# A two-block transformer kernel with split fp32 weights: three raw panel buffers instead of five, ten split ones instead of nine, and MoBA pairs computed in 512 columns

## What is computed

```
# first_block (two layers)
h = x
h = h + rmsnorm(gmlp_mixer(rmsnorm(h)))          # layer 0, stage GMLP
h = h + rmsnorm(conv_ffn(rmsnorm(h)))            # stage FFN0
h = h + rmsnorm(diff_attention(rmsnorm(h)))      # layer 1, stage DIFF
h = h + rmsnorm(conv_ffn(rmsnorm(h)))            # stage FFN1
# second_block
x = h + 0.5 * swiglu(rms_norm(h))                # stage FFN2
u = rms_norm(x) @ w_in                           # stage MIX
x = x + concat(mla_attention(u), moba_attention(u)) @ w_out
x = x + 0.5 * swiglu(rms_norm(x))                # stage FFN3
return rms_norm(x)

def conv_ffn(x):    # D_FF = 2816, causal depthwise conv of 3 taps
    g, u = split(causal_dwconv(x @ w_up))
    return (gelu(g) * u) @ w_down
def swiglu(x):
    return (silu(x @ w_gate) * (x @ w_up)) @ w_down
```

## Time and profile before

| | |
|---|---|
| median of 3 runs | 1059.04 us (1058.21 to 1059.07) |
| profiled execution | 1058.96 us |
| its span | 1056.8 us |
| PE busy | 1048.7 us (99%), 5806 matmuls |
| DVE busy | 776.3 us (73%) |
| ACT busy | 653.1 us (62%) |
| POOL busy | 49.7 us (5%) |
| DMA | 198.11 MB, mean 187 GB/s |
| granted TensorE clock | 1.00 |

### The profile page before, as it was taken

The page is one execution under the profiler, slowest core; times in us unless marked ns, Lnnn a source line. Parts: engine busy times, 40 slices in busy tenths (PEclk is TensorE's granted clock), DMA queues, the critical chain, the costliest instruction groups (busy, mean ns, idle before and its releaser), DMA issues.

```text
span 1056.8 us, 15343 instructions
## 1 busy us (share of the span) xinstructions
PE 1048.7 (99%) x5806; PEld 901.5 (85%) x5806; DVE 776.3 (73%) x1237; ACT 653.1 (62%) x1177; POOL 49.7 (5%) x45
## 2 busy tenths in 40 slices
PE   9999999999999999999999999999999999999997
PEld 7988888888888788888888888888898878888886
DVE  6788977888678889888887656655667867655664
ACT  6777756666667777666567555545556657444553
POOL 1910000000000000000000000000000000000000
PEclk9999999999999999999999999999999999999999
DMA  9764866655564257656554755666355536565641
GB/s 346 265 223 142 248 198 209 220 182 183 181 214 120 93 169 245 202 189 206 193 182 133 263 179 179 204 198 216 101 179 160 180 100 212 189 191 202 203 160 40
DMA packets 56776, 198.11 MB, mean 187 GB/s; under 512 B 6576, under 2 KB 8536, under 8 KB 56704
## 3 DMA queue, kind: packets, MB, share of 16 engines
q1 hardware_dynamic: 56160, 196.42, 56.5%
q10 hardware_dynamic: 432, 0.53, 0.1%
q0 software_dynamic: 112, 0.20, 0.1%
HBM read 195.35 MB, written 1.25 MB: 186 GB/s over the span
## 4 chain that ended last, share of the span: by engine, by line
PE 97%; DVE 1%; ACT 1%; issue 0%; POOL 0%; ACTq 0%; DVEq 0%; POOLq 0%
PE G L1485 31%; PE Y L1577 26%; PE G L1489 16%; PE G L1529 3%; PE G L1538 2%; PE G L1536 2%; PE G L1470 2%; PE Y L1572 2%; PE G L1471 2%; PE G L1472 2%; PE G L1551 1%; PE Y L1471 1%; PE Y L1472 1%; PE Y L1470 1%; PE G L1723 1%; PE Y L1601 1%
## 5 line engine op out<-in xcount | busy, mean ns | idle before, releaser
L928 DVE TENSOR_TENSOR w_low<-raw,w_high 128x1024 fp32r<-128x1024 f32 x346 | 417.4, 1224 | 35.2 <-ACT w_high L473 33.2
L473 ACT CAST w_high<-raw 128x1024 fp32r<-128x1024 f32 x351 | 362.7, 1045 | 13.3 <-DMA raw<-in_panels 8.4
L1485 PE MATMUL G<-x_parts,w_high 128*128 128x512 f32 x1408 | 352.5, 393 | 0.0
L1485 PEld LDWEIGHTS G<-x_parts,w_high 128*128 128x128 f32 x1408 | 257.1, 189 | 49.1 <-issue 0.7
L1489 PEld LDWEIGHTS G<-x_parts,w_low 128*128 128x128 f32 x1408 | 192.2, 191 | 13.7
L1489 PE MATMUL G<-x_parts,w_low 128*128 128x256 f32 x1408 | 196.4, 283 | 0.0
L574 ACT COPY big<-G 128x512 f32<-128x512 f32 x80 | 46.8, 585 | 226.4 <-PE G L1489 226.4
L1031 DVE TENSOR_TENSOR w<-G,big 128x512 f32<-128x512 f32 x80 | 55.2, 690 | 155.9 <-ACT big L574 155.8
L1577 PE MATMUL Y<-w_high,a_high 128*128 128x512 f32 x416 | 130.9, 396 | 1.0 <-DVE a_low L1297 1.0
L1577 PE MATMUL Y<-w_high,a_low 128*128 128x512 f32 x416 | 128.9, 391 | 0.0
L1577 PE MATMUL Y<-w_low,a_high 128*128 128x512 f32 x416 | 128.6, 390 | 0.0
(11 more groups left out here) (273 smaller groups left out, 1157.1 us busy)
## 6 DMA issues: line engine op xcount, KB each, us to landing
raw<-in_panels SPq DMA_DIRECT2D x352, 512.0 KB, 4.3
gain_pre<-in_gains SPq DMA_DIRECT2D x7, 512.0 KB, 5.5
gain_post<-in_gains SPq DMA_DIRECT2D x4, 512.0 KB, 6.4
big<-in_xT SPq DMA_DIRECT2D x4, 256.0 KB, 7.7
h<-in_x SPq DMA_DIRECT2D x2, 512.0 KB, 8.3
big<-rel_rows SPq DMA_DIRECT2D x8, 128.0 KB, 4.8
big<-in_w_s SPq DMA_DIRECT2D x1, 512.0 KB, 9.1
big<-in_b_s SPq DMA_DIRECT2D x1, 512.0 KB, 10.8
```

Source lines behind the costliest of these rows:

```text
L473: s.copy(WH[:, n % RING, :], raw[:, n % RAWS, :]).then_inc(hi, 1)
L928: v.tensor_tensor(WL[:, n % RING, :], raw[:, n % RAWS, :], WH[:, n % RING, :].bitcast(F32), ALU.subtract).then_inc(lo, 1)
L1485: mm(out, WH[:, n % RING, k * P:(k + 1) * P], X2[:, k, :, :], start=k == 0, stop=False, skip_group_check=True)
```

## The change

What it does:

1. `RAWS` goes from 5 to 3 and `RING` from 9 to 10. `load(n)` so waits for the split of panel n - 3, and the cast of panel n for PE's use of panel n - 10.
2. The cap of `share` goes up by one: 9 panels ahead on ACT, 8 on DVE. For the last eight features it is RING as before, now 10 and 9.
3. Panel DIFF+29 is split by POOL instead of DVE. POOL's helper falls in two, `at_boundary` with the wait on the rows and `low_part` without.
4. In the tail of DIFF the order on ACT and DVE is another: `upto(DIFF + 29)` on ACT comes before the squares of heads 6 and 7, `head_values(7)` on DVE before `low_head(4)`, and the last panels are cast one head later or earlier.
5. The MoBA q/k pairs go through `wide_tile` (banks G[:, 0] and G[:, 1]), and through `low_qk` on ACT and `sum_qk` on DVE. `qk_out` and its semaphore are gone, and the waits on it are waits on `dsum_r`. The banks of the latent queries, keys and values are renumbered.

The diff, cut to this:

```diff
-RAWS = 5
-RING = 9
+RAWS = 3
+RING = 10
...
-        BY_POOL = [STARTS[b] + 3 for b in range(1, 7)]
+        BY_POOL = [STARTS[b] + 3 for b in range(1, 7)] + [DIFF + 29]
...
-            def low_part(b):
-
-                n = STARTS[b] + 3
-                pool.wait_ge(xn_r, sixth(b, 0, 2))
+            def low_part(n):
                 pool.wait_ge(lo, n)
                 pool.wait_ge(hi, n + 1)
                 g.tensor_tensor(WL[:, n % RING, :], raw[:, n % RAWS, :], WH[:, n % RING, :].bitcast(F32),
                                 ALU.subtract).then_inc(lo, 1)
 
-            low_part(1)
+            def at_boundary(b):
+
+                pool.wait_ge(xn_r, sixth(b, 0, 2))
+                low_part(STARTS[b] + 3)
+
+            at_boundary(1)
             pool.wait_ge(rel_rd, 16 * 8)
             g.tensor_copy(bias[:, :, 0:P], bias[:, :, SC - P:SC]).then_inc(bias_r, 1)
-            for b in range(2, 7):
-                low_part(b)
+            at_boundary(2)
+            low_part(DIFF + 29)
+            for b in range(3, 7):
+                at_boundary(b)
...
-                todo = min(seen + (8 if f < NF - 8 else RING), PANELS - 1) + 1 - made[0]
+                todo = min(seen + (9 if f < NF - 8 else RING), PANELS - 1) + 1 - made[0]
...
 
-                act.wait_ge(used, DIFF + 9 + 2 * k + m)
+                act.wait_ge(used, (DIFF + 9 if k < HEADS else MIX - 5) + 2 * k + m)
                 if k:
                     act.wait_ge(dsum_r, 2 * (k - 1) + m + 1)
                 s.activation(qk_low[:, m, :], G[:, m, T:2 * T], ACT.Copy, scale=1.0 if m else DIFF_D ** -0.5)\
                     .then_inc(dlow_r, 1)
-
-            def qk_out(a):
-                act.wait_ge(used, MIX - 4 + 2 * a)
-                bank = G[:, (a - 7) % 2, :]
-                s.activation(qk[:, a % 2, 0, :], bank[:, 0:T], ACT.Copy, scale=DIFF_D ** -0.5)
-                s.copy(qk[:, a % 2, 1, :], bank[:, T:2 * T]).then_inc(qk_r, 1)
 
...
+            upto(DIFF + 29)
             high_head(3)
             squares_out(6).then_inc(ac, 1)
             rms_out(6, 7, 3)
-            high_head(4)
-            upto(DIFF + 29)
+            high_head(4), high_head(5)
             squares_out(7).then_inc(ac, 1)
             rms_out(7, HEADS, 4)
-            high_head(5)
+            upto(DIFF + 30)
+            high_head(6)
             upto(DIFF + 31)
-            for e in range(6, HEADS):
-                high_head(e)
-                upto(DIFF + 26 + e)
+            high_head(7)
+            upto(DIFF + 33)
 
             boundary(3, ACT.Gelu_apprx_tanh)
...
+            low_qk(9, 0)
             upto(B + 17)
-            qk_out(9)
-            turned_out(8, 0), turned_out(8, 1)
+            low_qk(9, 1)
+            turned_out(8, 0)
+            low_qk(10, 0)
+            turned_out(8, 1)
             upto(B + 18)
-            exps(9)
-            qk_out(10)
+            exps(9, lambda: low_qk(10, 1))
             cast(8)
...
             upto(B + 19)
             turned_out(9, 1)
             upto(B + 20)
             exps(10)
+            low_qk(11, 0)
             cast(9)
             upto(B + 21)
-            qk_out(11)
+            low_qk(11, 1)
...
-                s.activation(mlaV[:, t, :], G[:, 1 - t, :], ACT.Copy, scale=rtc[:, 2 + t:3 + t]).then_inc(mlav_r, 1)
+                s.activation(mlaV[:, t, :], G[:, t, :], ACT.Copy, scale=rtc[:, 2 + t:3 + t]).then_inc(mlav_r, 1)
...
-                todo = min(seen + (7 if f < NF - 8 else RING - 1), PANELS - 1) + 1 - made[0]
+                todo = min(seen + (8 if f < NF - 8 else RING - 1), PANELS - 1) + 1 - made[0]
...
             norm_head(5)
+            head_values(7)
             low_head(4)
             inverse_rms(6, 7, 3)
             norm_head(6)
-            head_values(7)
-            upto(DIFF + 29)
             low_head(5)
...
             dve.wait_ge(cb_r, 1)
+            sum_qk(9, 0)
+            upto(B + 16)
+            sum_qk(9, 1)
             upto(B + 17)
+            sum_qk(10, 0)
 
...
-                if a < HEADS:
+                if a < 12:
                     pe.wait_ge(dsum_r, 2 * a + 2)
-                elif a < 12:
-                    pe.wait_ge(qk_r, a - HEADS + 1)
...
-                if j < 2:
-                    pe.wait_ge(v_r, 6 - j)
-                else:
-                    pe.wait_ge(qk_r, j - 1)
                 for m in range(2):
-                    tile_out(B + 10 + 2 * j + m, G[:, (j + 1) % 2, m * T:(m + 1) * T])
+                    if j:
+                        pe.wait_ge(dsum_r, 2 * (HEADS + j - 1) + m + 1)
+                    else:
+                        pe.wait_ge(v_r, 5 + m)
+                    wide_tile(B + 10 + 2 * j + m, G[:, m, :])
                     if m == 0 and between is not None:
                         between()
 
...
-                    pe.wait_ge(qk_r, 3 + u)
+                    pe.wait_ge(dsum_r, 2 * HEADS + 7 + u)
                 else:
```

More of the change, by code:

```diff
@@ L242, in build_program @@
         ah, al = sem("a_high_r"), sem("a_low_r")
-        v_r, qk_r, sc_r, nm_r, ex_r, at_r, T_r, pt_r, pv_r, ov_r, ss_r, ot_r = (
-            sem(n) for n in ("v_r", "qk_r", "scores_r", "negmax_r", "exp_r", "attn_r", "turned", "turned_r",
+        v_r, sc_r, nm_r, ex_r, at_r, T_r, pt_r, pv_r, ov_r, ss_r, ot_r = (
+            sem(n) for n in ("v_r", "scores_r", "negmax_r", "exp_r", "attn_r", "turned", "turned_r",
                              "pv_r", "ov_r", "ss_r", "out_turned"))
@@ L853, in _ @@
             upto(B + 15)
-            qk_out(8)
+            low_qk(8, 0), low_qk(8, 1)
             act.wait_ge(cms, 1)
@@ L1120, in combine, with pair_weights @@
                 v.tensor_reduce(nm[:, b, 2:4], out[:, :, P:SC], AX_X, ALU.max, negate=True).then_inc(nm_r, 1)
-            def pair_weights(a):
+            def pair_weights(a, between=None):
                 b = a % 2
@@ L1131, in pair_weights @@
                     last.then_inc(an_r, 1)
+                    if m == 0 and between is not None:
+                        between()
             def weigh(a):
@@ L1382, in _ @@
             upto(B + 14)
+            sum_qk(8, 0), sum_qk(8, 1)
             dve.wait_ge(cl_r, 5)
@@ L1419, in _ @@
             upto(B + 18)
-            pair_weights(9)
+            pair_weights(9, lambda: sum_qk(10, 1))
             combine(10)
@@ L1424, in _ @@
             pair_weights(10)
+            sum_qk(11, 0)
             low_out(9)
             upto(B + 21)
+            sum_qk(11, 1)
             queries(0)
@@ L1920, in mla_q @@
                             ready(n)
-                        last = product(G[:, (7 + u) % 2, m * T:(m + 1) * T], n % RING, blk % 8 * P, P,
+                        last = product(G[:, u % 2, m * T:(m + 1) * T], n % RING, blk % 8 * P, P,
                                        CH[k], CL[k], k == 0, k == 2)
@@ L1937, in mla_k @@
                     for k in range(2):
-                        last = product(G[:, (11 + u) % 2, m * T:(m + 1) * T], n % RING,
+                        last = product(G[:, u % 2, m * T:(m + 1) * T], n % RING,
                                        ((u % 2 * 2 + m) * 2 + k) * P, P, CH[3 + k], CL[3 + k],
@@ L1951, in mla_v @@
                         hic, loc = WH[:, j, half(k)], WL[:, j, half(k)]
-                        mm(G[:, 1 - t, :], xh, hic, start=k == 0, stop=False)
-                        mm(G[:, 1 - t, :], xh, loc, start=False, stop=False)
-                        last = mm(G[:, 1 - t, :], xl, hic, start=False, stop=k == 1)
+                        mm(G[:, t, :], xh, hic, start=k == 0, stop=False)
+                        mm(G[:, t, :], xh, loc, start=False, stop=False)
+                        last = mm(G[:, t, :], xl, hic, start=False, stop=k == 1)
                 last.then_inc(used, 1)
```

4 lines of the change are left out of this document (2 added, 2 removed).

## The result

The changed kernel took **1147.36 us** in the median of 4 runs (1146.45 to 1152.58), against 1059.05: 1.0844 times as long, with a 95% interval of 1.0831 to 1.0857, or 88 us slower. Medians and differences in this document leave out two runs that fell in a slower state, one of 1256.51 us (experiment 7) and one of 3702.28 us (experiment 11). The prediction had the sign and the kind of loss right (1105, range 1068 to 1128), but about half its size: the result lies outside the range.

What follows compares the result with a forecast made beforehand. PE was taken to bound the kernel, 99% busy. Terms 1.5 + 17.2 + 2 + 0 + 17.2 + 2.2 + (4.6 - 0.9) + 2.2 = +46.0 us on about 1059 gave 1105 us, range 1068 to 1128.

Steps and rivals of the forecast that it cites:

- The bound and the loop: Whole kernel and conv FFNs: PE bounds before; three raw buffers close a loop through ACT, DVE and SP's loads, 8.8 us.
- 0.5 us per step more than PE's 8.31: Conv FFN steps of three panels: the raw loop sums to 8.86, called 8.8 us, so each step loses this.
- The size of a conv FFN: FFN0 and FFN1: late start plus accumulating loops, less end slack, cost 17.2 us each.
- From there I add loops: FFN0 from the split at 116.7: 4 x 6.5, 7 x 8.8, 10.1 and 6 x 8.8 lead to 267.2.
- slack at the end: End of a conv FFN: PE's last d panel began 1.55 us after the last hidden low part, taken off 18.7.
- one cast's worth, 10.1: Conv FFN step f = 14: the cap grows by one, two casts stand ahead of the tap, step 10.1 us.
- bounds: nothing, and one landing of 3.5: Start of GMLP: fourth load behind the first split, two parts of x behind that load; taken as +1.5 us.
- The stop for the latent values: MIX: load of B+30 waits for the split of B+27, so PE waits for the mlaV copies, +4.6 us.
- The SwiGLU FFNs: FFN2 and FFN3: only the start is late; PE's g(4) waits 2.2 us for the sum of f = 2 in each.
- late copy of `first_two`: Start of FFN0: ACT's second such copy stands behind a late cast and PE waits for it, about 1 us.
- The clock: Whole kernel, rival, chance 0.11: granted clock falls after about ten PE stops, +28 us on top, 1133 us.
- The tail of DIFF and the pairs: DIFF's tail: -0.9 and about +1.0, together 0; MoBA pairs in MIX: eight panels by `wide_tile`, -0.9 us.

Runs made afterwards that it cites:

- experiment 7: Kernel before with five raw buffers, but loads of GMLP's panels wait for the split of n - 3 as if three: 1070.35 us, 1.0107.
- experiment 11: Kernel before with the MoBA pairs in 512 columns, plus share's caps raised to 9 and 8, five raw buffers: 1060.38 us, 1.0015.
- experiment 5: Changed kernel with last tap and hidden tile's high part ahead of all casts of the step on ACT in conv FFNs: 1107.76 us, 1.0468.
- experiment 13: Changed kernel itself, unedited, run again beside another run on the same chip: 1146.65 us.
- experiment 12: Changed kernel with unread matmuls filling PE's idle time in FFN0 and FFN1, ahead of g(4) and the waits for f = 20 and 21: 1149.28 us, 1.0865.
- 14: Changed kernel with 9 unread matmuls ahead of PE's waits for hidden tiles f = 19 and 20 in both conv FFNs: 1149.16 us.

## Why the prediction was wrong, point by point

- **The bound and the loop: right.** "0.5 us per step more than PE's 8.31" was 8.9 in the steady steps of FFN1, for 8.8. With two panels the forecast was 6.5 and the steps are 6.6. Three buffers alone make 80 of 88 us, and the loops were undone by order alone (experiment 5).
- **The size of a conv FFN: 17.2 against 29.1 and 26.2.** The step that failed is the one of "From there I add loops": its sum of the chain puts one loop of 8.8 in every step of three panels, and takes off 1.55 of slack at the end. For FFN1, by taps:

| piece of FFN1 | forecast | measured |
|---|---|---|
| entry, to the tap or split of f = 2 | 6.0 | 7.3 |
| f = 2 to 6 | 4.5 | 5.7 |
| f = 6 to 13 | 3.5 | 5.9 |
| f = 13 to the last tile | 4.8 | 7.0 |
| slack at the end | -1.5 | +0.3 |

  From f = 6 to 7 the step is 10.46 (taps at 483.29 and 493.75). ACT's timeline there shows a second loop, which I had not seen:

```profile
483.29 1.09 ACT L606 ACTIVATE w<-w,par 128x256 f32<-128x256 f32 x2 [0.23 <-DVE w L1032]
486.27 1.05 ACT L477 CAST w_high<-raw 128x1024 fp32r<-128x1024 f32 x1 [1.89 <-DMA raw<-in_panels]
487.23 0.40 ACT L582 CAST a_high<-w 128x256 fp32r<-128x256 f32 x1
```

  The second cast waits 1.89 us for its load, and the hidden high part stands behind it. The low part (DVE, 487.66), its split (488.00) and the load for the cast of 492.80, issued at 489.25, follow from that. I had followed the first cast of a step and not the other two. At f = 14 two casts stand ahead of the tap, and each waits for its own load:

```profile
555.69 1.05 ACT L477 CAST w_high<-raw 128x1024 fp32r<-128x1024 f32 x1 [3.15 <-DMA raw<-in_panels]
...
558.35 1.05 ACT L477 CAST w_high<-raw 128x1024 fp32r<-128x1024 f32 x1 [1.60 <-DMA raw<-in_panels]
559.30 1.09 ACT L606 ACTIVATE w<-w,par 128x256 f32<-128x256 f32 x2
```

  The step is 11.94, where I had added one cast's worth, 10.1, and not a second landing. The slack of 1.55 was measured at tile f = 21, but PE waits at f = 19 and 20, so it takes nothing off. The lower clock then ate the time between f = 20 and the end (4.29 for 2.72 us in FFN0).
- **FFN0: 3 us more than FFN1.** Its steps are 8.9 to 10.9 long. I had taken one landing of 3.5 from a quiet step, and the median of 3.7 from a stretch of FFN1. In FFN0 the median was 4.1 before (110 to 250 us) and is 4.3 now. That the table rows, which SP loads in this stage alone (`rel_rows`), are the reason is argued, not shown.
- **GMLP: 1.5 against 11.2, the largest error.** The step "bounds: nothing, and one landing of 3.5" was wrong: I had costed only SP's first loads and never laid the three-buffer wait over the rest of the stage. Some of the lateness is from the start, more than the 1.5: ACT came to the squares of the rows at 29.51, where it was 25.34 before, 4.2 us late. The rest shows as a chain in mid-stage, where the cast of a panel stands ahead of ACT's root for the layernorm:

```profile
46.02 1.05 ACT L477 CAST w_high<-raw 128x1024 fp32r<-128x1024 f32 x1 [3.24 <-DMA raw<-in_panels]
...
48.49 0.28 ACT L719 ACTIVATE lnsd<-lnmv,eps 128x2 f32<-128x2 f32 x1
```

  The cast waits 3.24 us for a load that could only go out behind DVE's splits of 39.58 (the chain has it under way from 40.86 to 45.94), and the root (L719) comes at 48.49, where it was 38.89 before, now 9.6 us late. PE has stopped for 6.19 us when it goes on at 67.75. Experiment 7 bears the stage's loss out: 11.4 us.
- **MIX: 3.7 against 7.0.** The stop for the latent values was 4.49 us for the 4.6 forecast. Windows over DIFF and MIX, from the end of the stage before to their own, before and after (columns: stretch, its length, busy time and instructions of PE, PEld, DVE, ACT, POOL, granted clock, DMA share, GB/s):

```profile
257.05:370.23 113.18, 112.13 (x629) 93.28 (x628) 89.68 (x182) 80.28 (x205) 2.39 (x1) 1.00 0.47 153
...
738.90:858.99 120.09, 120.09 (x835) 105.38 (x834) 87.65 (x163) 73.12 (x163) 2.41 (x1) 1.00 0.46 151
```
```profile
297.31:416.53 119.22, 114.95 (x630) 94.51 (x628) 89.75 (x180) 79.87 (x204) 4.77 (x2) 0.98 0.46 146
...
815.16:942.22 127.06, 122.57 (x771) 104.25 (x770) 90.78 (x171) 73.28 (x162) 2.41 (x1) 0.97 0.46 141
```

  MIX lost 7.0 us: 4.5 of stop, and 2.5 in which PE was busy longer with 64 matmuls fewer. That the clock is on the path there can be seen in the change run again (experiment 13). There the granted clock in MIX (815.95 to 942.36) was 0.99 and PE was busy 121.13 us, 1.4 less, and without its stop for the values the stage was shorter by as much (126.41 - 5.28 = 121.1, here 127.06 - 4.49 = 122.6). In DIFF PE was busy 2.8 us longer, and one stop of 2.44 us at 340.69 (PE behind DVE's sum of a q/k tile) was not forecast. The SwiGLU FFNs lost 3.8 and 4.4 for 2.2: PE's stop at g(4) was 2.52 and 3.10, and ACT's late copy of `first_two`, which I had named for FFN0 and left out here, stopped PE for another 0.80 and 0.75 (at 652.59 and 966.02).
- **The clock: a rival that came true beside the forecast.** It was given a chance of its own at +28 us, and PE's busy time did grow by 27.4. But that is no 28 us of the total: at g(4) a faster PE gained nothing (experiment 12), at the ends of the two stages about 2 us each (14), and in MIX and DIFF up to the 2.5 and 2.8 us above. That the number came out near the rival's +28 is luck: it had taken ten returns of 2.8 us each, all on the path. The Trainium skill (TensorE: Matmul & The Clock Gate, "HAM oscillation — how this bites in real kernels") has a matmul engine that waits for DMA between bursts start the next one cold. Here it waits for other engines' results. This trace agrees in most places and not in all: after 3.16 us at 271.71 eight matmuls took 2.12, after 1.93 at 235.86 they took 3.52.
- **The tail of DIFF and the pairs.** Forecast 0 and -0.9, measured together with five buffers as no difference.
- **The caps.** Costed only as part of the late starts that three buffers make. They cost about 2 us with five buffers too, and 2.5, not clear of the spread, with three.

Where the 88 us are, then: 55 in the two conv FFNs, 11 in GMLP, 21 in the other four stages. By cause 80 are the three buffers' and about 2 the caps'. The last 6 (the change without its caps, 1144.9, against three buffers alone, 1138.7) stay open. Both kernels vary by 5 to 8 us from run to run, their intervals just touch (1.0796 to 1.0836, and 1.0734 to 1.0797), and their profiled runs took 1145.1 and 1145.2. Ten split buffers alone, and the new tail of DIFF with three raw ones, were not run.

## What to carry to other kernels

When a buffer count falls, draw for every use of the buffer the way from the load's landing to the instruction that frees it, in each engine's own order, and add up the loop against the step of the engine that sets the pace: what stands between a waiting instruction and the freeing one counts in full, on every engine that it passes. Follow all places of a step and all stages, not the one that looks tightest. Before giving back a buffer, move the instructions that others need ahead of those that wait for a load: two calls were worth 40 us here.

## What the runs showed of the hardware

A load of 512 KB took 3.3 us from issue to landing at the least in the changed kernel (3.2 before), and 3.6 (MIX) to 4.6 (GMLP) in the median of a stage. With three buffers three panels per 8.31 us came through (experiment 5). In the changed kernel the granted clock fell after stops of PE of 1.93 to 6.19 us, not after each of them (after 3.16 and 3.10, at 271.71 and 978.17, it held), and once it stayed down for all of the eight matmuls of 512 columns that followed (3.78 us at 456.12). The kernel before, bound by PE, repeated within 1 to 2 us (1058.35 to 1059.14 in nine runs). The kernels with three raw buffers in all stages, where loops through loads set the pace, varied by 4 to 9.
